# The same steps in another order: which step of which job each engine takes next in a two-block transformer layer pair

## The reference, cut to what matters

```python
h = rms_norm(x, pre_norm_w)
p = h @ w_in                                   # 1024 x 8320 columns
# recurrent branch, 8 heads of 64: for each token
sa = einsum('bhvk,bhk->bhv', state, a_t)
state = state * w_t + sa * b_t + v_t * k_t
y_t = einsum('bhvk,bhk->bhv', state, r_t)
# the branches' outputs, gated and projected
proj = einsum('nbsc,ncd->nbsd', [y_a, y_b, y_c], w_branch)
x = x + rms_norm(sum_n(sigmoid(gate_n) * proj_n) @ w_out, post_norm_w)
```

```python
n = rms_norm(h, attn_norm_w); proj = n @ w_in_2
h = h + concat([attention(q, k, v), silu(rg) * norm(retention(rq, rk, rv))]) @ w_out_2
m = rms_norm(h, ffn_norm_w_2)
h = h + (silu(m @ w_gate) * (m @ w_up)) @ w_down
```

## Time and profile before

| | |
|---|---|
| median of 3 runs | 2267.68 us (2266.09 to 2271.28) |
| the profiled execution: its time | 2262.68 us |
| the profiled execution: first to last instruction (span) | 2260.9 us |
| mean granted TensorE clock | 0.995 of full |
| PE busy | 2226.6 us |
| DVE busy | 1540.7 us |

### The profile page before, as it was taken

How to read it: one execution, slowest core, us unless ns; L and a number is a source line. 1 busy time by engine, 2 the same in 40 slices (tenths; PEclk the granted TensorE clock), 3 DMA queues, 4 the chain that set the end, 5 groups by cost and what they waited for, 6 DMA issues and landing times.

```text
span 2260.9 us, 31568 instructions
## 1 busy us (share of the span) xinstructions
PE 2226.6 (98%) x12344; PEld 1842.1 (81%) x12344; DVE 1540.7 (68%) x2562; ACT 828.5 (37%) x1436; POOL 599.9 (27%) x465
## 2 busy tenths in 40 slices
...
GB/s 154 47 56 43 65 56 41 60 51 56 60 76 123 121 112 146 287 186 125 103 67 51 52 48 56 39 131 103 85 75 84 84 84 84 84 108 120 98 91 176
DMA packets 249316, 208.59 MB, mean 92 GB/s; under 512 B 44624, under 2 KB 218320, under 8 KB 249168
## 3 DMA queue, kind: packets, MB, share of 16 engines
...
## 4 chain that ended last, share of the span: by engine, by line
PE 84%; DVE 9%; DMA 2%; issue 2%; ACT 1%; POOL 1%; SPq 1%; DVEq 0%; ACTq 0%
PE PS L120 81%; PE PS L123 3%; DVE acc L129 1%; DMA wSrcA<-in_w_down_dram 1%; DVE Nn L129 1%; DVE Ntmp L129 1%; DVE wSrcS L129 1%; SPq L146 1%; POOL wLoA L129 1%; DVE wLoS L129 1%; DVE ST L137 1%; DMA Wraw<-in_w_in_dram 0%; DVE ot L129 0%; DVE Zt L129 0%; POOL wLoS L129 0%
## 5 line engine op out<-in xcount | busy, mean ns | idle before, releaser
L120 PE MATMUL PS<-Hhi,Whi 128*128 128x512 f32 (+1 forms) x1304 | 422.7, 391 | 4.3 <-DVE Hlo L129 2.7
L120 PE MATMUL PS<-Hhi,Wlo 128*128 128x512 f32 (+1 forms) x1304 | 421.2, 390 | 0.0
L120 PE MATMUL PS<-Hlo,Whi 128*128 128x512 f32 (+1 forms) x1304 | 421.2, 390 | 0.0
L120 PEld LDWEIGHTS PS<-Hhi,Whi 128*128 128x128 f32 x1304 | 240.6, 190 | 50.8 <-issue 6.3
L120 PEld LDWEIGHTS PS<-Hhi,Wlo 128*128 128x128 f32 x1304 | 242.2, 190 | 45.9 <-issue 1.6
L120 PEld LDWEIGHTS PS<-Hlo,Whi 128*128 128x128 f32 x1304 | 242.1, 190 | 46.0 <-issue 1.4
L126 ACT ACTIVATE Whi<-Wraw 128x512 fp32r<-128x512 f32 x170 | 106.7, 629 | 392.7 <-PE PS L120 388.5
L129 POOL TENSOR_TENSOR Wlo<-Wraw,Whi 128x512 fp32r<-128x512 f32 x82 | 121.2, 1479 | 414.7 <-ACT Whi L126 414.4
L129 DVE TENSOR_TENSOR Ntmp<-Nn 32x30 f32<-32x30 f32 (+14 forms) x240 | 90.3, 376 | 24.3 <-DMA Nn<-scr_ns 17.7
L129 DVE TENSOR_TENSOR Nn<-Nn,Ntmp 32x30 f32<-32x30 f32 (+14 forms) x240 | 93.5, 389 | 6.7
L129 DVE TENSOR_TENSOR Wlo<-Wraw,Whi 128x512 fp32r<-128x512 f32 x88 | 65.0, 742 | 29.2 <-ACT Whi L126 28.3
...
## 6 DMA issues: line engine op xcount, KB each, us to landing
Wraw<-in_w_in_dram SPq DMA_DIRECT2D x126, 256.0 KB, 2.9
...
```

Of the source, the lines that this page charges most:

```text
L120: return self.h.matmul(out, lhsT, rhs, start=start, stop=stop, skip_group_check=True)
```

## The change

Only `ORDER` and `PICKS` change: the letters of each engine are the same in number, 4,350 on PE, 2,372 on DVE, 1,268 on ACT, 425 on POOL and 553 on SP, and every step does the same work. Where short steps of the recurrent branch stood directly behind each other, pairs of the dense product now stand between them. In the first block's stretch with recurrent units PE goes from a dense pair to a short step 137 times before and 171 times after, for the same 232 short steps; in the attention stretch 131 and 122 times, for 221. The start, the gates, the projections and the feed-forward keep their order on PE but for the last sixteen transposes. A piece of PE's string, units 0 to 2:

```diff
-        "a5d29a2d7a2d2a2d13adad18a2d13a2d113pd4pd8pd19id3pd19s2d2s2d3id4pd4pd8pd17id72pd3id4s3d3s2d2s2d2scsd2"
-        "csdscds2cd2pcd3cd3cd4cd23gd6pd11pd15s3dpds2d4sd4sd4csdcd3cdicd2s2d3cs2dcsd2cicd3pd4pd14gpd16id69pd4i"
+        "a5d30a2d7a2dad10ad7a2d15a2d14a2d116pd9pd12pd17id4id7s2d3s2d7pd8pd9pd16pd22id25id8psd3sdsd5s2d2sdsdsd"
+        "csdsdcsdscsd2cd3cdpcd3cd3cd23gd18sd5spd5sd5psdsd3s2d6scsdcd2icd3idcd3cd2pcd3cd3cd6sd2sd2sdsd7gd8pd9p"
```

More of the change, by code:

```diff
@@ L3125 @@
[L3125 to L3129, removed]
@@ L3142 @@
-    "dve":
[L3143 to L3160, removed]
@@ new lines @@
+        "a5d30a2d7a2dad10ad7a2d15a2d14a2d116pd9pd12pd17id4id7s2d3s2d7pd8pd9pd16pd22id25id8psd3sdsd5s2d2sdsdsd"
+        "csdsdcsdscsd2cd3cdpcd3cd3cd23gd18sd5spd5sd5psdsd3s2d6scsdcd2icd3idcd3cd2pcd3cd3cd6sd2sd2sdsd7gd8pd9p"
+        "d14pd21id23id7spd4s2d5s2d2sdsdsdcsdcds2dcd2scsd2cd3cdpcd3cd21gd21sd5spd5sd5s2d2sdsdsd2csdcd3cpd2cd3c"
+        "d3cd3cd2icd3id10psd3s2d3sgd9pd10pd17pd23id23id7s2d4sdpd3s2d2sdsdsdcsdcds2dcds2cd3cd4cpdcd3cmd4md11gd"
+        "33sd2sdsd5psd3s2d2sdsdcsdcd3cpd2cd3cd3cd3cd2icd3id10psd3s2d3sgd9pd10pd5m2d9pd23id39m2d4id6sdsd2sd3pd"
@@ new lines @@
+        "sdsd3s2d2scdsdcds2cd2scsd2cmdmcd3cd3cd24gd31s2d4sd5s2d2sdsdsdcsdcd5cd4cd3cd4cd3cd3cd46gd692n2d14n2d1"
+        "4n2d14n2d24n2d24n2d24n2d43n2d106kd5v2d6k2d35kd33v2d2td2rd3xdrdrd3tdtd2yrdx2d4wdtyd4xyd14t2d3rd10wrtd"
+        "xd2kxd2ydtd3trd12ry2d3wxd3yd16v2rd4xdr2xd3wtdrdy2d5xd2tdtd4wtxd3xyd8t2d4rd11kry2d3rwdxryd10xdxydydwt"
+        "d3xd9t2kwtdxd4xyd7k2d2rd5v2dtdtdr2yd3yd3rwxd6yd7x2d5y2wtd6xd9rd3kd6rt2d2x2wrd3ydrdtdkd5t2yd2yd3k2wxk"
+        "dyd9k2xd4xd3rwtyd4xyd5v2dtd3txdrwtdrd2xd5ryd6t2d9y2d3wxd12rd14r2dxd2xdrwd3kd12k2d117n2d9n2d11n2d9n2d"
@@ new lines @@
+        "25n2d24n2d24n2d36n2d1014o2do2d15odod5o2d8ododo2d10o4",
+    "act":
+        "q2w2awa3q4awaqa3qa8w2ewe2wp2wp3wepwpwes2ws2wfp5w2fpwpw3fsws6wfs6pwgwfwgwep4sws2wesps3ps2w2esgws3gwp3"
+        "wp2wfpwpwfw2fsws8ws4pwgwfgw2ep2sp2sws4wes3pwpwegsws3gwfp5w2fpwpw3fs2ws9wfs2pwfgfwfgw2ep4ws6wes3pwpwe"
+        "gsws3gwfp5wf2wfpwpwfw3f3wfs7ws6f2wfwgwfgfw2f2s2ws6wfsfw2fgwfwtwTSgwtSTtS4tSTtSTS3t3S2tStS4tSt2S2t2S5"
+        "t3S2t2S5t3S2t2S5t3S2t2S5t3S2t2S5t3S2t2S5t3S2t2S5t3S2t2b3wbwtwt2wtw2bwbwb2w4b2wlwblw2bw5mwm2wmwm3wmwm"
+        "3wm2wm3n3h2n2h2n2h2nh2n2h2n2h2n2h2n2h2r3k2w3v3kw2kwk2wowkwvkv2wx2ryxyxy2zwzoz2x3wy2xwk2ycrwyx4z2wozk"
+        "r2zr2kwy2wvyz2v2zyrwcx2zx2woy4x3wz2xwk2zrzcr2ywyz2yzr2ykzkwx2okxy2xycwykx2wxvz2vzvxrzwy3woz2yz2cwx2w"
+        "k2xy3rxykwk2r2z2rx2zxrxzkwokcy2kywz2yz2xwxvxy2vxvy2rcwx3wxoz4wywydwyrdyrkcwdkdw3i2wdi2wd2i2di2n2h4n2"
+        "h4nh2nh2nh2nh2Sw2uwS2TwTS2uSTS2uTS5u2S2uS4uSuS2uS4uSuS2uS4uSuS2uS4uSuS2uS4uSuS2uS4uSuS2uS4uSuS2uS4uS"
+        "uS2uS4uSuS2uS4uSuS2uS4uSuS2uS4uSuS2uS4uSuS2uS4uSuS2uS4uSuS2uS4uSuS2uS4uSuSuw2uwuwH3SH2SHuS5H7SuSu2H2"
+        "S4uSuSuH5uSuH2S4uSuHSHuH3u2SHuS5u2SuHuSuHS5H3uHSH2SH3S5H2SH2S7H5SHS6HSH5S6H2SH3S5H2SH2S7H5SHS6HSH5S5"
+        "HS21",
```

64 lines of the change are left out of this document (35 added, 29 removed).

## The result

| | before | changed |
|---|---|---|
| median | 2267.24 us (2264.72 to 2272.12, 6 runs) | 2255.72 us (2252.38 to 2258.70, 6 runs) |
| ratio, 95% interval | | 0.9944 [0.9929, 0.9960] |
| the profiled execution | 2262.68 us | 2258.70 us |
| its mean granted clock | 0.995 | 0.996 |

The change makes the kernel 11.5 us (0.5%) faster. The profiled execution shows only 4.0 us of that, since before's profile caught a short execution and this one the longest of its six. So the trace is read by stretches, and two more profiles of the changed kernel are used beside it.

What follows compares the result with a forecast made beforehand. PE, busy 98% of the span, bounds the kernel; only its idle time and low clock can be gained. -8.5 - 3.9 - 5.5 + 3 + 2 = -12.9, say -12.5 us, laid on the 2267.68 us median: 2255.2 us, range 2247 to 2265.

Steps and rivals of the forecast that it cites:

- low stretches: Recurrent stretch, 40 to 720 us: five places where PE's clock falls below 1.00; all predicted to go, -8.5 us.
- idle time of PE: First block: WU bank waits -3.9 us, other waits -5.5, inversion coming due +3, tighter DVE order +2.
- extra switches: 34 more runs of short steps in the first block, 9 fewer in attention; +0.5 us at most, taken as 0.
- full narrow run: Recurrent units: X11t, WU,AB and X22c in a row without a dense pair, claimed enough to lower the clock in some cases.
- 1.31 us wait: Units 1, 3 and 5: PE idle between two WU,Tt steps sharing one bank; three waits predicted to go, -3.9 us.
- `X11t` in units 3 and 7: Inversion's step in the recurrent stretch: PE predicted to arrive early and wait about 1 us for its DMA in each.
- tight: Recurrent stretch, DVE: new order as tight as the old, which had 5.5 us of other waits; +2 us, from 0 to +6.
- A: Rival: clock falls as often, there or elsewhere; only 4 us gained, 2263.7 us; chance 0.10.
- C: Rival: slower, X11t coming 2.8 us after PE in each of eight units, ending above 2272 us; chance 0.05.
- B: Rival: PE runs into X11t in every unit and idle there lowers the clock anew; +6 us, 2261; chance 0.15.
- D: Rival: all gained, nothing comes due; 17.9 us off, 2249.8 us; chance 0.20.
- The attention stretch: Stretch behind the gates: PE waits 0.9 us in all there; change taken as 0, from -1 to +3 us.

## Why the prediction was right, point by point

**The number.** 2255.2 us was predicted, 2255.72 measured. For the profiled execution it had 2250.2 us; the three profiles are 2258.70, 2252.23 and 2252.26. The mechanism was right, but that the number is met within 0.5 us is luck: over all executions the gain is 14.1 us in the mean. The clock gave 1.7 us more than the five low stretches (10.2 for 8.5), the switches cost 2.8 us that were taken as nothing, and the new waits have the right sum from another place. A slip in the working: its chances of faster, same and slower (0.85, 0.11 and 0.05) add up to 1.01.

| term, first block | predicted | first profile |
|---|---|---|
| low stretches | -8.5 | -8.5 |
| idle time of PE: -3.9 - 5.5 + 3 + 2 | -4.4 | -4.9 (11.9 to 7.0) |
| extra switches | 0 | +2.8 |
| sum, to the first gate block | -12.9 | -10.6 (673.1 to 662.5) |

The third row was not measured by itself: it is what is left of the sum. The other two profiles give -11.8 and -11.2 for it.

**Clock.** The five low stretches are gone in all three profiles, as predicted. The reason given, that each follows the full narrow run or the 1.31 us wait, is shown by undoing one at a time: either brings low stretches back, each of about 1.7 us, the wait alone in four of eight places and the narrow run alone in three of seven in the new order (six of seventeen with the old order's profiles). Why a place has one in one case and not in the next stays open. The Trainium skill (TensorE: Matmul & The Clock Gate, section Why this matters for your kernels) ties a drop in mid-kernel to idle gaps between bursts of matmuls. The gaps that its row means are longer than any in the first block, so by it none of the five low stretches would have been there; the prediction stretched it to the waits of 1.31 us. By either reading joining the narrow steps again would have brought nothing; it brought four, three of them with PE busy throughout, and so the measurement decides against that rule as the only one. That the median gains more than the profile of before shows (10.2 us of clock for 8.5) is what the prediction allowed for when it laid its difference on the median: before's profile is one of its shorter executions.

**The waits that went.** The three on ACT's `WU` (3.9 us), the last `g` step's (1.4), `AB`, `cy` and `cu` (2.4) and the gate block's (0.8) are all gone; on `Xs` 0.7 of 1.7 us are.

**The waits that came.** The amount was right (4.5 us on `WU` and `Yt` for 3 + 2), the place was not, so the amount was met by luck. The prediction had PE idle for 1 us ahead of `X11t` in units 3 and 7, waiting for its DMA. There is no such wait. In unit 3 PE comes 2.0 us closer behind `BK` than before (54.95 for 56.90 us from the end of `RAV,BK`), not 3.3, since the 1.60 us on `WU` at 296 us fall in between; `X11t` has landed 1.2 us before. What is late is DVE's list of copies and sums, 29 us ahead of `X11t`, not the inversion. That was the part of the sum called "tight", and it made most of the new waits.

**The step that was mis-sized** is "Extra switches": taken as 0, at most +0.5 us, it comes out at 2.8, as what is left of the sum. The prediction counted only that a pair behind a short step takes longer, 0.45 + 0.09 us. A pair between two narrow steps takes 0.66 us, 0.21 more than among its like. The new order parts the narrow steps at 13 of the 16 places, and 13 x 0.21 = 2.7 us (an estimate, with the price of the run that parted them in the old order). That joining them again gave back about 3 us agrees with it.

**Rivals.** A (the clock stays low as often) is out, as the first block has no low stretch in any of three profiles, and C (slower) is out by the time. B (the inversion decides) is out by its place: no wait on `X11t` in any unit. D (everything gained, 17.9 us) is too much, for the medians and for the mean of 14.1 us. **The attention stretch**, put at 0 (from -1 to +3), gives no difference in the times; in single profiles it is 1.5 to 4.6 us longer than in the one of before, which is the shortest of its order.
